# Attention exponentials written over their input, and reciprocal sums spread by DVE before PE turns them

## The reference

```
score = index_scores(qib, ki, wib, qpos, kpos)        # picks the 256 keys of each query
s = einsum('bqhgd,bqnhd->bqhgn', qg, ks) * 64 ** -0.5
s = where(valid, s, -inf)
p = softmax(s, axis=-1)
o = einsum('bqhgn,bqnhd->bqhgd', p, vs)
```

## Time and profile before

| | |
|---|---|
| median of 3 runs | 3597.99 us (3596.61 to 3599.53) |
| the profiled execution | 3597.02 us, span 3595.3 us |
| PE busy | 3460.8 us (96%) |
| PE weight loads (PEld) | 3266.6 us (91%) |
| DVE busy | 2039.3 us (57%) |
| POOL busy | 1545.4 us (43%) |
| ACT busy | 770.5 us (21%) |
| chain that ended last | PE 90%, DVE 4%, POOL 2%, issue 2%, ACT 2%, DMA 1% |

### The profile page before, as it was taken

The page is one execution under the profiler, slowest core; times in us unless marked ns, Lnnn a source line. Parts: engine busy times, 40 slices in busy tenths (PEclk is TensorE's granted clock), DMA queues, the critical chain, the costliest instruction groups (busy, mean ns, idle before and its releaser), DMA issues.

```text
span 3595.3 us, 57385 instructions
## 1 busy us (share of the span) xinstructions
PE 3460.8 (96%) x22646; PEld 3266.6 (91%) x22646; DVE 2039.3 (57%) x3072; ACT 770.5 (21%) x1585; POOL 1545.4 (43%) x675
## 2 busy tenths in 40 slices
PE   8999999998999999999888889999999999999998
PEld 7999999998986999999767747879999999999998
DVE  5333333346666999987776644995283533324334
ACT  2000000012232111133576523762100200000000
POOL 3533443432322444444357513984444343453351
PEclk9999999999998999999799977999999999999999
DMA  2111111112211222232233236953351111111111
GB/s 91 53 47 35 53 53 35 46 47 78 56 31 47 89 95 90 84 97 90 60 100 89 80 86 159 244 145 96 107 175 51 40 55 35 42 57 41 41 54 57
DMA packets 392979, 272.33 MB, mean 76 GB/s; under 512 B 54970, under 2 KB 368650, under 8 KB 392856
## 3 DMA queue, kind: packets, MB, share of 16 engines
q1 hardware_dynamic: 373032, 225.76, 22.2%
q10 hardware_dynamic: 19824, 44.95, 3.3%
HBM read 211.05 MB, written 59.81 MB: 75 GB/s over the span
## 4 chain that ended last, share of the span: by engine, by line
PE 90%; DVE 4%; POOL 2%; issue 2%; ACT 2%; DMA 1%; ACTq 0%; DVEq 0%; SPq 0%; POOLq 0%
PE setA L365 10%; PE setA L366 10%; PE setB L365 10%; PE setA L367 10%; PE setB L366 10%; PE setB L367 10%; PE bankC L365 2%; PE bankC L367 2%; PE bankC L366 2%; PE bankD L367 2%; PE bankD L365 2%; PE bankD L366 2%; PE setB L517 1%; PE bankC L1498 1%; PE bankD L2118 1%
## 5 line engine op out<-in xcount | busy, mean ns | idle before, releaser
L345 POOL TENSOR_TENSOR whi<-wraw,ones 128x1024 fp32r<-128x1024 f32 x190 | 471.8, 2483 | 1634.3 <-PE setA L367 1044.2
L365 PE MATMUL setA<-hhi,whi 128*128 128x352 f32 (+1 forms) x2304 | 752.6, 327 | 20.8 <-POOL wlo L348 10.0
L365 PE MATMUL setB<-hhi,whi 128*128 128x352 f32 (+1 forms) x2304 | 747.9, 325 | 1.9 <-POOL wlo L348 1.9
L366 PE MATMUL setA<-hlo,whi 128*128 128x352 f32 (+1 forms) x2304 | 746.8, 324 | 0.0
L367 PE MATMUL setA<-hhi,wlo 128*128 128x352 f32 (+1 forms) x2304 | 745.8, 324 | 0.0
L366 PE MATMUL setB<-hlo,whi 128*128 128x352 f32 (+1 forms) x2304 | 743.0, 322 | 0.0
L367 PE MATMUL setB<-hhi,wlo 128*128 128x352 f32 (+1 forms) x2304 | 741.7, 322 | 0.0
L348 POOL TENSOR_TENSOR wlo<-wraw,whi 128x1024 fp32r<-128x1024 f32 x190 | 475.8, 2504 | 14.9
L365 PEld LDWEIGHTS setA<-hhi,whi 128*128 128x128 f32 x2304 | 437.2, 190 | 27.8 <-issue 18.5
L365 PEld LDWEIGHTS setB<-hhi,whi 128*128 128x128 f32 x2304 | 434.0, 188 | 6.3 <-POOL wlo L348 2.5
L366 PEld LDWEIGHTS setA<-hlo,whi 128*128 128x128 f32 x2304 | 437.0, 190 | 1.7
(11 more groups left out here) (423 smaller groups left out, 5716.2 us busy)
## 6 DMA issues: line engine op xcount, KB each, us to landing
wraw<-in_w_in SPq DMA_DIRECT2D x64, 512.0 KB, 3.7
wraw<-in_w_ffn_gate SPq DMA_DIRECT2D x44, 512.0 KB, 3.8
wraw<-in_w_ffn_up SPq DMA_DIRECT2D x44, 512.0 KB, 3.8
wraw<-in_w_ffn_down SPq DMA_DIRECT2D x44, 512.0 KB, 3.6
abc<-acsD SPq DMA_DIRECT2D x8, 2048.0 KB, 10.9
xcD<-cv ACTq DMA_DIRECT2D x24, 520.0 KB, 2.7
zD<-spill ACTq DMA_DIRECT2D x16, 524.0 KB, 2.7
sraw<-sD SPq DMA_DIRECT2D x2, 4192.0 KB, 13.1
```

Source lines behind the costliest of these rows:

```text
L345: pool.tensor_tensor(dst_cols(slot, hi), dst_cols(slot), ones[:, :].unsqueeze(1).to_broadcast([P, KD, P]), ALU.mult).then_inc(w_hi, 1)
L365: pe.matmul(out, w1, r1, start=start, stop=False)
L366: pe.matmul(out, w1, r2, start=False, stop=False)
```

## The change

- `smx` takes the exponentials in place: `pr` is gone, PE turns `smx`, mask(u) waits for the transposes of unit u - ahead instead of for its exponential, and ACT's exponential loses its wait for those transposes.
- The reciprocals are spread by DVE: after the reciprocal (and a wait for its end) a copy writes `rlx` [128, 8, 64], each sum 64 times. PE then turns two heads at once, [128, 128], by one transpose: 4 instead of 8 matmuls.
- `ptT` moves to where `pr` lay, `rlx` lies behind it, and an unused tile keeps the tensors behind at their addresses.

```diff
-        pr = a.take("pr", [P, 2, L])
         ptT = a.take("ptT", [P, 4, NT, P])
+        rlx = a.take("rlx", [P, 8, HD])
+        a.take("spare", [P, 8320 // 4 - 8 * HD])
...
                         mm = pe.transpose(CD[bank][0:kn, b * P:(b + 1) * P],
-                                          buffer(pr, u, (b0 + b) * P, (b0 + b) * P + kn), ident[:, :])
+                                          buffer(smx, u, (b0 + b) * P, (b0 + b) * P + kn), ident[:, :])
...
                 for k in range(n):
-                    for h in range(2):
-                        mm = pe.matmul(bankC[h * HD:(h + 1) * HD, k * P:(k + 1) * P],
-                                       rl[:, 2 * k + h:2 * k + h + 1].to_broadcast([P, HD]), ident[:, :],
-                                       start=True, stop=True)
+                    mm = pe.transpose(bankC[:, k * P:(k + 1) * P],
+                                      rlx[:, 2 * k:2 * k + 2, :].rearrange("p h d -> p (h d)"), ident[:, :])
...
                 act.wait_ge(s_masked, u + 1)
-                if u >= ahead(u):
-                    wait_both(act, pt_done, u - ahead(u) + 1)
...
-                act.activation(buffer(pr, u, 0, w), buffer(smx, u, 0, w), ACT.Exp, bias=nmax[:, u % 4:u % 4 + 1],
+                act.activation(buffer(smx, u, 0, w), buffer(smx, u, 0, w), ACT.Exp, bias=nmax[:, u % 4:u % 4 + 1],
...
                 if u >= ahead(u):
-                    v.wait_ge(exp_done, u - ahead(u) + 1)
+                    wait_both(v, pt_done, u - ahead(u) + 1)
...
-                v.reciprocal(rl[:, 0:n], lsum[:, i // 2 % 2, i % 2 * 8:i % 2 * 8 + n]).then_inc(rl_ready, 1)
+                ch.run(v.reciprocal(rl[:, 0:n], lsum[:, i // 2 % 2, i % 2 * 8:i % 2 * 8 + n]))
+                v.tensor_copy(rlx[:, 0:n, :], rl[:, 0:n].unsqueeze(2).to_broadcast([P, n, HD])).then_inc(rl_ready, 1)
```

## The result

The changed kernel takes 3610.99 us (median of 6 runs, 3609.75 to 3612.73) against 3596.23 (3590.80 to 3599.53): a ratio of 1.0040, 95% interval 1.0029 to 1.0050. It is about 14.8 us slower. The forecast was 3611, in a range of 3598 to 3618. The profiled execution has a span of 3609.2 us, 13.9 more than before.

What follows compares the result with a forecast made beforehand. PE, busy 96% of the span, was taken to bound the kernel, with most turns waiting for DVE's reciprocal. Gains 1.7 against losses 15.5, mostly copies waiting for POOL: net 13.8 slower on 3597.0, forecast 3611, range 3598 to 3618.

Steps and rivals of the forecast that it cites:

- Exponential in place: DVE's masks and ACT: the new wait is met by the order of work, the dropped wait was redundant; value 0.
- The copy stands still beside POOL: DVE's spread copy waits until POOL's running instruction ends, then takes about 0.3 us; chance 0.83.
- Rival 1: The spread copy does not wait for POOL: 3596 to 3599 us, no change; chance 0.13.
- the subtraction k2lo: DVE subtraction taken as evidence of the wait: 3.52 us, ending 0.56 behind POOL's end.
- Group 11: Copy comes at about 1958.55, after POOL's start at 1958.23, and waits until 1962.8: 4.2 us lost, plus clock 2.4.
- Rival 2: Group 11's copy slips in ahead of POOL's instruction: 6.6 us less, 3604 to 3605; chance 0.28 within the POOL wait.
- Groups 12 and 13: Group 12's delay falls into DVE's existing wait for POOL; group 13's turn comes at 2014.2: 2.5 us lost.
- Rival 3: Group 13's copy falls into POOL's next instruction: 4.5 us more, 3616; chance 0.22 within the POOL wait.
- Clock: PE's granted clock falls to half after the stalls: 1.8 us charged for group 6, 2.4 for group 11.
- group 6: Copy waits for POOL until 1865.62, turn 3.5 us late: 3.0 us lost net, plus clock 1.8.
- group 4: Turn 1.8 us late beside POOL, but DVE's next subtraction waits for POOL anyway: 0.1 us lost.
- The saving on PE: Turn by 4 transposes instead of 8 matmuls: 0.49 us less per group at full clock, offset by 0.47 of copy delay.

Runs made afterwards that it cites:

- e2: Kernel before with only the exponential in place, its mask waiting for the transposes and ACT's wait gone: 3597.64 us, ratio 1.0005 to the kernel before.
- e1: Changed kernel with the reciprocals spread by a sum over one element (TENSOR_REDUCE) instead of a copy: 3600.07 us, ratio 1.0014 to the kernel before.
- e3: Changed kernel with POOL's state update of sample rows 2 to 7 cut to one sixteenth of its elements: 3597.55 us.
- e9: e7 with the last tile's reciprocal and spread back in their old place and ACT's copy_out ahead of the exponential: 3590.04 us, ratio 0.9981 to the kernel before.
- e7: e1 with reciprocal and spread first in DVE's order of the unit, ahead of bankD's copy: 3600.70 us, ratio 1.0013 to the kernel before.
- e6: Kernel before with only the reciprocal moved ahead of bankD's copy in DVE's order: 3596.81 us, ratio 1.0000.
- e10: e6 with the last tile's reciprocal back in its old place and ACT's copy_out ahead of the exponential: 3590.88 us, ratio 0.9986 to the kernel before.
- e5: Changed kernel with reciprocal and spread copy first in DVE's order of the unit, ahead of bankD's copy: 3613.84 us, ratio 1.0045 to the kernel before.
- e8: Changed kernel with the copy and its wait kept, but the turn done by the 8 matmuls as before: 3619.12 us, ratio 1.0058 to the kernel before.

## Why the prediction was right

The table compares the terms. The measured cost of a group is the growth of the reciprocal's shift (start after less start before) until the next group's reciprocal. Groups 5, 9, 14 and 15 are left out; they were forecast at nothing and measure 0.0 to 0.1.

| group | predicted | measured |
|---|---|---|
| ahead of the stage | 0 | +0.5 |
| 0 to 3 | -1.2 | -1.0 |
| 4 | +0.1 | -1.3 |
| 6 | +3.0, clock +1.8 | +4.9 |
| 7 | -0.2 | 0.0 |
| 8 | +0.9 | +1.1 |
| 10 | +0.65 | +0.7 |
| 11 | +4.2, clock +2.4 | +4.9 |
| 12 and 13 | +2.5 | +2.2 |
| last | -0.3 | -0.2 |
| behind the stage | 0 | +2.0 |
| sum | +13.8 | +13.9 |

- *Exponential in place: 0.* Shown by e2 within its interval. In the changed kernel no mask waited for PE's transposes, only 22.4 us for the scores (20.4 before).
- *The copy stands still beside POOL.* Shown from both sides: other instruction (e1), other POOL work (e3). Rival 1 is out. The rule of the Trainium skill's page SBUF — State Buffer (SBUF: two separate sides) held for a source with a zero step too, with copies of 1.33 to 4.43 us. The one-source reduction of e1 took 0.69 us and did not wait; by the Trainium skill's page VectorE: DVE Perf Modes (The perf-mode tier table) a reduction has only the one-element mode, and so it is not under that rule. The prediction put the subtraction k2lo (3.52 us) under the two-port mode as well. It has two tensors as inputs, and the same section of the Trainium skill's page SBUF — State Buffer names that case apart: a VectorE instruction with two inputs in SBUF, against a GpSimd instruction that reads SBUF.
- *Group 11.* The copy came 0.36 us into POOL's instruction; 0.3 was forecast. Rival 2 is out by that margin. The way there was as forecast: from group 10 to 11 the reciprocal fell 0.7 us further behind, POOL's instructions 0.1.
- *Groups 12 and 13.* The turn of group 13 came 0.34 us behind POOL's end, as forecast. The delay of groups 11 and 12 used up the 2.57 us for which DVE had waited; that wait is gone from the trace. But it did not cover all of group 12: 1.6 us arose there and 0.65 in group 13, where 0 and 2.5 were forecast. Rival 3 did not happen: the copy began 1.5 us ahead of POOL's end.
- *Clock.* About right behind group 6 (3 us at 0.50, 3 at 0.72: 1.5 + 0.8 lost; 1.8 was charged, and the group's total is 0.1 off). Too high behind group 11: 2 us at 0.67 and 3 at 0.65 lost 1.7, of which the group's total leaves some 0.7. In group 4 I missed a gain: before, PE ran at 0.50 from 1843; now the same stretch shows 1.00. That is about the 1.3 us. I had priced the collision's stall there, not where the idle times then lie. Nor is one idle time enough to tell the clock: PE stood for 2.62 us ahead of that stretch before and for 2.63 now, and only before did the clock fall. What set it is not shown.
- *The saving on PE* (0.49 a group, eaten by 0.47 of delay): groups 5, 7, 9, 14 and 15 measure 0.0 to 0.1. The turn took 0.66 us instead of the 0.60 taken, so 0.43 was saved and not 0.49. That copy_out was a limit in wide groups, as said, the 7.5 us of e9 over e7 show.

The collisions came as forecast, but that the total hit 3611.0 so closely is luck. Misses cancel: 3.1 us too much in groups 4 and 11, 2.5 too little outside the stage. And the medians differ by 14.8 us, 1.0 more than forecast, from a kernel before that is 0.8 below the 3597.0 on which the sum was built.

## What to carry to other kernels

Before a small DVE instruction goes between two engines, look at what POOL runs at that moment: a copy of 0.43 us made the stage up to 4.9 us longer (groups 6 and 11). A one-source reduction over one element does the same copy in 0.69 us and did not wait. And ask what is late next: by the traces, the saved PE time was worth nothing until ACT's copy_out, which a wait of 12.3 us in the table had named, was moved too (up to unit 120, e7 is 1.1 us behind e6, and e9 is 4.4 ahead of e10).

## What else the runs showed

- Five of the six kernels whose turn uses the 66 transposes (the changed one, e1, e3, e5, e7) show 787.8 to 788.3 us from the last residual addition to the last output copy; the sixth, e9, and all six with 132 matmuls show 785.9. In the changed kernel it is one output slot that came free later (3.53 us of waiting instead of 1.51). Two DVE rows of the tail, the kernel before first:

```profile
3588.49 0.69 DVE L2529 COPY yout<-setA 128x512 f32<-128x512 f32 x1 [1.51 <-DMA out_y_prompt<-yout]
```

```profile
3602.42 0.69 DVE L2527 COPY yout<-setA 128x512 f32<-128x512 f32 x1 [3.53 <-DMA out_y_prompt<-yout]
```

- The cause stays open; no run tried it. In the same way e8 and e10 are 2.5 us shorter in SSD (163.3 and 163.4 us from the last copy of the final states to the first sum of the mix, 165.6 to 166.0 in the ten others).
- A DVE copy that waits while a POOL instruction ends goes ahead of POOL's next one. All seven ended 0.27 to 0.29 us behind the first; in six of them POOL had its next instruction ready, and the trace shows it begun between 0.04 us ahead of the first one's end and 0.08 behind it. No copy had to let a second one pass.
